# Chunk steps without Q in a hybrid trunk kernel: the inverse goes into b and r_b once, and dense pieces lie in 8 gaps

## What is computed

```python
kk = hd(k * k_k)
kk = kk / jnp.maximum(jnp.linalg.norm(kk, axis=-1, keepdims=True), 1e-12)
k = k * (1 + (a - 1) * k_a)
b_h = kk * a_h
def step(state, inp):          # one token, 16 heads of 64
    r_t, w_t, k_t, v_t, kk_t, b_t = inp
    sa = jnp.einsum('bhvk,bhk->bhv', state, -kk_t)
    state = state * w_t[:, :, None, :] + sa[..., None] * b_t[:, :, None, :] + v_t[..., None] * k_t[:, :, None, :]
    return state, jnp.einsum('bhvk,bhk->bhv', state, r_t)
_, y = lax.scan(step, state0, xs)
y = group_norm(y) * g_lnx + b_lnx
bonus = jnp.sum(r_h * k_h * r_k, -1, keepdims=True) * v_h
return ((y + bonus) * g) @ w_ob
```

## Time and profile before

| | us |
|---|---|
| median of 3 runs | 1109.28 |
| lowest, highest | 1109.05, 1109.8 |
| the profiled execution | 1107.22 |
| its span in the profile | 1105.4 |
| TensorE busy | 1077.7 |
| VectorE busy | 802.7 |
| ScalarE busy | 569.6 |
| GpSimd busy | 72.2 |

### The profile page before, as it was taken

One profiled execution on the slowest core, in us unless ns is written; L12 is line 12 of the kernel. 1 busy time (PEld: TensorE's weight loads), 2 busy tenths in 40 slices (PEclk: granted clock), 3 DMA queues, 4 the chain that ended last, 5 costly groups with the idle time before them and its releaser, 6 DMA issues. The chain is left out here.

```text
span 1105.4 us, 31915 instructions
## 1 busy us (share of the span) xinstructions
PE 1077.7 (97%) x13568; PEld 977.2 (88%) x13568; DVE 802.7 (73%) x1471; ACT 569.6 (52%) x1008; POOL 72.2 (7%) x61
## 2 busy tenths in 40 slices
PE   8999999999999999999999999999999999999996
PEld 8878888888997999998898888888888979999885
DVE  3678787868676877774557887878876778777645
ACT  3653555555544555553246445555565445555531
POOL 0000010101001000000100000202011010000001
PEclk9999999999999999999999999999999999999998
DMA  8533232322564666566474323222326637566661
GB/s 302 166 102 118 72 101 80 95 90 89 191 229 135 211 190 189 186 200 197 134 236 142 121 88 98 89 86 81 98 64 229 210 128 226 189 185 189 210 188 56
DMA packets 45526, 165.58 MB, mean 150 GB/s; under 512 B 5168, under 2 KB 5424, under 8 KB 45136
## 3 DMA queue, kind: packets, MB, share of 16 engines
q1 hardware_dynamic: 42736, 154.03, 43.4%
q0 software_dynamic: 1504, 7.47, 2.2%
q10 hardware_dynamic: 1152, 2.10, 0.6%
HBM read 160.44 MB, written 3.15 MB: 148 GB/s over the span
## 5 line engine op out<-in xcount | busy, mean ns | idle before, releaser
L771 PE MATMUL ps<-x_tok_r,mid_hi 128*128 128x256 f32 x576 | 177.1, 307 | 0.5 <-DVE ring_r L1758 0.5
L773 PE MATMUL ps<-x_tok_r,ring_r 128*128 128x256 f32 x576 | 162.2, 282 | 0.0
L772 PE MATMUL ps<-yb_hi,mid_hi 128*128 128x256 f32 x576 | 162.1, 281 | 0.0
L1758 DVE TENSOR_TENSOR ring_r<-ring,mid_hi 128x1024 fp32r<-128x1024 f32 x80 | 97.2, 1216 | 31.1 <-ACT mid_hi L1342 31.0
L771 PEld LDWEIGHTS ps<-x_tok_r,mid_hi 128*128 128x128 f32 x576 | 108.5, 188 | 9.5 <-issue 1.4
L772 PEld LDWEIGHTS ps<-yb_hi,mid_hi 128*128 128x128 f32 x576 | 108.9, 189 | 0.7 <-issue 0.7
L773 PEld LDWEIGHTS ps<-x_tok_r,ring_r 128*128 128x128 f32 x576 | 108.9, 189 | 0.0
L1342 ACT CAST mid_hi<-ring 128x1024 fp32r<-128x1024 f32 x80 | 83.8, 1048 | 34.3 <-PE ps L773 26.6
L2021 DVE TENSOR_TENSOR rs_ks_r<-ring,tha_kkn_r 128x1024 fp32r<-128x1024 f32 x44 | 53.9, 1224 | 19.9 <-ACT tha_kkn_r L1394 19.7
L2021 DVE TENSOR_TENSOR vs_dC_r<-ring,b_k_r 128x1024 fp32r<-128x1024 f32 x44 | 53.7, 1220 | 17.6 <-ACT b_k_r L1394 17.6
L2021 DVE TENSOR_TENSOR X_Y_r<-ring,arc_r 128x1024 fp32r<-128x1024 f32 x42 | 51.3, 1222 | 19.8 <-ACT arc_r L1394 19.8
(11 more groups left out here) (487 smaller groups left out, 3326.0 us busy)
## 6 DMA issues: line engine op xcount, KB each, us to landing
ring<-stream_dram SPq DMA_DIRECT2D x281, 512.0 KB, 3.7
lora_w<-lora_dram POOLq DMA_DIRECT2D x2, 1536.0 KB, 7.2
W_bt<-rpar_dram POOLq DMA_DIRECT2D x4, 512.0 KB, 5.1
kt_V<-rpar_dram POOLq DMA_DIRECT2D x4, 512.0 KB, 7.1
x_tok<-x_dram SPq DMA_DIRECT2D x2, 512.0 KB, 4.7
v_saved_dram<-vs_dC ACTq DMA_DIRECT2D x4, 256.0 KB, 4.5
x_tok<-x_dram SPq DMA_DIRECT2D x1, 1024.0 KB, 6.2
vf<-v_saved_dram ACTq DMA_DIRECT2D x4, 256.0 KB, 3.8
```

The source lines that it names most:

```text
L771: pe.matmul(dst, lh, rh, start=start, stop=False)
L772: pe.matmul(dst, lh, rl, start=False, stop=False)
L773: return pe.matmul(dst, ll, rh, start=False, stop=stop)
L1758: dve.tensor_tensor(rounded["ring"][:, k, :], ring[:, k, :], f32(mid_hi[m % NM][:, :]), ALU.subtract).then_inc(*dve_mid.inc(l, m))
```

## The change

**No Q.** The last level of the inverse now updates X and leaves Y (the update on VectorE takes the other half of the block). After it one block, `byX`, multiplies X into b for six units (all but the last chunk's) and into r_b for eight, and does the products of r and the keys with V for all eight units. ScalarE copies the results back over `bt` and `rb` (`by_x`, four copies); `rkv_out` is called once, at the second chunk. A chunk step is then Z, and S with y straight from `Zs`. TensorE has 9690 matmuls where it had 9594, ScalarE 966 instructions where it had 982, VectorE 1433 for 1441, GpSimd 93 for 65.

**Gaps.** A round has 23 gaps, 0 to 22: 14 is ahead of `byX`, 15+2c behind Z, 16+2c behind S. The 20 pieces (19 in the last round of a layer) lie in gaps 14 to 21.

**Orders of casts and subtracts.** `mids_up_to` is called twice a chunk on both engines, without the condition on the chunk.

**Norms and bonus.** The norm's power is split on GpSimd into a rounded high part and the rest, both are transposed, and two rounded products of 256 columns spread them (`spread` holds the selecting rows of both). The bonus product is two rounded ones of 512 columns: ScalarE makes the high part (`bonus_high`), GpSimd the low one (`bonus_low`), which needs ScalarE's.

**Decay.** `d_ext` keeps the exponential of the cumulative sum in columns 1 to 64 of each unit with a 1 in column 0, so that the value before a token and the value at it are two views of it; the subtract at L1790 and the exponential at L1421 go.

```diff
-CHUNK_GAPS = ([[14, 14, 14, 15, 17, 17, 18, 18, 19, 19, 20, 20, 21, 21, 22, 22, 23, 23, 24, 24]] * (GROUPS - 1)
-              + [[14, 14, 15, 16, 16, 17, 17, 18, 19, 19, 20, 20, 21, 22, 22, 23, 23, 24, 24]])
+CHUNK_GAPS = ([[14, 14, 14, 15, 15, 16, 16, 17, 17, 18, 18, 18, 19, 19, 19, 20, 20, 20, 21, 21]] * (GROUPS - 1)
+              + [[14, 14, 15, 15, 16, 16, 16, 17, 17, 18, 18, 18, 19, 19, 19, 20, 20, 21, 21]])
...
-GAPS = 14 + 3 * NCH
+GAPS = 15 + 2 * NCH
...
+                whole = rn[:, :].rearrange("p (t j) -> p t j", t=TT)
+                pool.wait_ge(*pool_prep(r, "rn"))
+                pool.tensor_copy(rn_hi, whole).then_inc(*pool_prep.inc(r, "rn_hi"))
+                pool.wait_ge(*pool_prep(r, "rn_hi"))
+                pool.tensor_tensor(rn_lo, whole, f32(rn_hi), ALU.subtract).then_inc(*pool_prep.inc(r, "rn_lo"))
+
+            def bonus_low(r):
+
+                pool.wait_ge(*act_rkk(r, "hi"))
+                pool.tensor_tensor(rkk_lo, flat(tmp), f32(rkk_hi), ALU.subtract).then_inc(*pool_rkk.inc(r, "lo"))
...
+                    bonus_low(r)
+                    if g:
+                        y_rstd(r - 1)
+                        y_out(r - 1)
                     if g + 1 < GROUPS:
...
             def prep_rnT(r):
-                pe.wait_ge(*pool_prep(r, "rn"))
-                pe.transpose(bank(4)[0:8, 128:256], rn[:, :], ident).then_inc(*pe_prep.inc(r, "rnT"))
+                pe.wait_ge(*pool_prep(r, "rn_lo"))
+                for t in range(TT):
+                    mm = pe.transpose(bank(4)[0:8, P + t * P:2 * P + t * P], rn_parts[:, 8 * t:8 * t + 8], ident)
+                mm.then_inc(*pe_prep.inc(r, "rnT"))
 
             def prep_rnx(r):
 
                 pe.wait_ge(*dve_prep(r, "rnT"))
+                pe.wait_ge(exact, 2)
                 for b in range(GB):
-                    for t in range(TT):
-                        j = TT * b + t
-                        mm = pe.matmul(tok(4)[:, b, t * P:t * P + P], C["rowsel"][0:8, j * P:j * P + P], rnT[:, :],
-                                       start=True, stop=True)
+                    mm = pe.matmul(tok(4)[:, b, :], spread[:, b * P:b * P + P], rnT, start=True, stop=True)
                 mm.then_inc(*pe_prep.inc(r, "rnx"))
...
-                pe.wait_ge(*dve_prep(r, "rkk"))
+                pe.wait_ge(*pool_rkk(r, "lo"))
                 pe.wait_ge(*(act_y(r - 1, "yn") if g else dve_att(l, f"lh{g}")))
-                pe.matmul(bank(6), C["bones"], flat(tmp), start=True, stop=True).then_inc(*pe_bonus.inc(r, "bonus"))
+                pe.matmul(bank(6), bones_r, rkk_hi, start=True, stop=False)
+                pe.matmul(bank(6), bones_r, rkk_lo, start=False, stop=True).then_inc(*pe_bonus.inc(r, "bonus"))
...
+                fill(14, 1)
+                pe.wait_ge(*dve_wkv(r, f"X{LEVELS - 1}1"))
                 pe.wait_ge(*act_wkv(r, "ktV"))
+                if g + 1 < GROUPS:
+                    pe.wait_ge(*act_prep(r + 1, "thw"))
+                early = sum([bc(c) for c in range(NCH // 2)], [])
+                late = sum([bc(c) for c in range(NCH // 2, NCH)], [])
+                for i in range(len(early) + NU):
+                    if i < len(step_units):
+                        u = step_units[i]
+                        per_head(unit64(3)[:, u, :], X, bt[:, u, :], u)
+                    elif i < len(step_units) + len(late):
+                        u = late[i - len(step_units)]
+                        per_head(unit64(5)[:, u, :], X, rb[:, u, :], u)
+                    if i < len(early):
+                        u = early[i]
+                        mm = crossed(unit64(2)[:, u, :], X, rb[:, u, :], u)
+                    else:
+                        u = i - len(early)
+                        mm = swapped(rkv64(u % NCH)[:, u // NCH, :], rk[:, u, :], Vc[:, u, :])
+                mm.then_inc(*pe_wkv.inc(r, "byX"))
                 for c in range(NCH):
-                    if c:
-                        pe.wait_ge(*dve_wkv(r, f"S{c - 1}"))
-                    s_old = S[:, (c + 1) % 2, :, :]
                     y = [unit64(5)[:, u, :] for u in bc(c)]
                     if c:
+                        s_old = S[:, (c + 1) % 2, :, :]
+                        pe.wait_ge(*dve_wkv(r, f"S{c - 1}"))
                         for b, u in enumerate(bc(c)):
                             mm = per_head(step64(2)[:, b, :], a_of, s_old[:, b, :], u)
                             if b == GB - 1:
                                 mm.then_inc(*pe_wkv.inc(r, f"Z{c}"))
                             crossed(y[b], r_of, s_old[:, b, :], u, start=(b == 0), stop=False)
-                    fill(14 + 3 * c, c == 0)
-                    pe.wait_ge(*dve_wkv(r, f"Z{c}" if c else f"Y{LEVELS - 1}1"))
-                    if c == 0 and g + 1 < GROUPS:
-                        pe.wait_ge(*act_prep(r + 1, "thw"))
-                    if c == NCH - 1:
-                        pe.wait_ge(*act_wkv(r, "rkV_first"))
-                    for b, u in enumerate(bc(c)):
-                        swapped(rkv64(c)[:, b, :], rk[:, u, :], Vc[:, u, :])
-                        mm = per_head(step64(3)[:, b, :], Y, Zs[:, b, :] if c else akV[:, u, :], u)
-                    mm.then_inc(*pe_wkv.inc(r, f"Q{c}"))
-                    fill(15 + 3 * c)
+                    fill(15 + 2 * c)
                     if g + 1 < GROUPS and c == 0:
                         prep_v(r + 1)
                         prep_rnT(r + 1)
-                    pe.wait_ge(*act_wkv(r, f"Q{c}"))
+                    pe.wait_ge(*(dve_wkv(r, f"Z{c}") if c else act_wkv(r, "rbX")))
                     for b, u in enumerate(bc(c)):
+                        z = Zs[:, b, :] if c else akV[:, u, :]
                         if c < NCH - 1:
-                            mm = per_head(step64(2)[:, b, :], bt, Qs[:, b, :], u)
+                            mm = per_head(step64(2)[:, b, :], bt, z, u)
                             if b == GB - 1:
                                 mm.then_inc(*pe_wkv.inc(r, f"S{c}"))
-                        mm = crossed(y[b], rb, Qs[:, b, :], u, start=(c == 0), stop=(c == 0 or b == GB - 1))
+                        mm = crossed(y[b], rb, z, u, start=(c == 0), stop=(c == 0 or b == GB - 1))
                     mm.then_inc(*pe_wkv.inc(r, f"y{c}"))
                     if g + 1 < GROUPS and c == 0:
                         prep_rnx(r + 1)
-                    fill(16 + 3 * c)
+                    fill(16 + 2 * c)
...
-                act.wait_ge(*dve_prep(r, "cp"))
-                act.activation(flat(dA), flat(dB), ACT.Exp, scale=-DECAY).then_inc(*act_prep.inc(r, "P"))
-                act.activation(flat(dC), flat(dC), ACT.Exp, scale=-DECAY).then_inc(*act_prep.inc(r, "Pp"))
+                act.wait_ge(*dve_prep(r, "cum"))
+                act.activation(d_at, by_unit(dB[:, :, :]), ACT.Exp, scale=-DECAY).then_inc(*act_prep.inc(r, "P"))
                 act.activation(flat(dB), flat(dB), ACT.Exp, scale=DECAY).then_inc(*act_prep.inc(r, "iP"))
...
+            def bonus_high(r):
+
+                act.wait_ge(*dve_prep(r, "rkk"))
+                act.copy(rkk_hi, flat(tmp)).then_inc(*act_rkk.inc(r, "hi"))
...
-            def chunk(r, c):
-                act.wait_ge(*pe_wkv(r, f"Q{c}"))
-                act.copy(Qs[:, :, :], step64(3)).then_inc(*act_wkv.inc(r, f"Q{c}"))
...
+            def by_x(r):
+
+                act.wait_ge(*pe_wkv(r, "byX"))
+                dst, src = [t.rearrange("p (b c) s -> p b c s", b=GB)[:, :, 0:NCH - 1] for t in (bt, unit64(3))]
+                act.copy(dst, src).then_inc(*act_wkv.inc(r, "btX"))
+                dst, crossed, own = [t.rearrange("p (b c) s -> p b c s", b=GB) for t in (rb, unit64(2), unit64(5))]
+                for q, o in zip(HEADS, OTHER):
+                    act.copy(dst[q, :, 0:NCH // 2], crossed[o, :, 0:NCH // 2])
+                act.copy(dst[:, :, NCH // 2:], own[:, :, NCH // 2:]).then_inc(*act_wkv.inc(r, "rbX"))
+
+            def rkv_out(r):
+
+                src = ps[:, 7, :].rearrange("p (c b s) -> p c b s", b=GB, s=CH)
+                dst = yt[:, :, :].rearrange("p (b c) s -> p c b s", b=GB)
+                for q, o in zip(HEADS, OTHER):
+                    last = act.copy(dst[o], src[q])
+                last.then_inc(*act_wkv.inc(r, "rkV"))
...
-                        mids_up_to(l, mids_by(GAPS * g + 13 + 3 * c))
+                        mids_up_to(l, mids_by(GAPS * g + (14 + 2 * c if c else 13)))
                         for kind, i in pairs_done(g, c=c - 1):
                             if kind == "gate":
                                 gate(l, i)
                             elif kind == "rkv":
                                 rkv(l, g + 1, i % 3)
-                        chunk(r, c)
+                        if c == 0:
+                            by_x(r)
+                        mids_up_to(l, mids_by(GAPS * g + 15 + 2 * c))
                         if c == 0 and nxt:
                             prep_exp(r + 1)
```

(45 more changed lines are left out.)

82 lines of the change are left out of this document (44 added, 38 removed).

## The result

The changed kernel took 1115.8 us in the median (1114.9 to 1117.3, 4 runs) against 1109.2 for the kernel before (1107.8 to 1109.8, 4 runs): a ratio of 1.0081, with a 95% interval of 1.0063 to 1.0099. Measured again beside the last experiment, with six runs, it was 1.0095 (1.0077 to 1.0113). It is slower: the medians lie 6.7 and 9.9 us apart, where 1.4 was forecast. The profiled execution of after took 1117.3 (span 1115.5), that of before 1107.2 (span 1105.4).

What follows compares the result with a forecast made beforehand. TensorE's queue was taken to bound the kernel. Stages -1.6, turns +3.3 and +4.95, bonus -3.2, last rounds -1.2 and first preparations -0.9 gave +1.4 on 1109.3: 1110.7 us, range 1102 to 1118.

Steps and rivals of the forecast that it cites:

- own case: Whole kernel: the prediction's main forecast, 1110.7 us, its own range 1107.5 to 1113.5, chance 0.45.
- the unit prices: TensorE timeline costs: run of 12 dense matmuls 1.62 us, 16 small ones 0.39; with nothing late the stage takes 22.15.
- The chunk stage: Gap 14 to end of y3, six rounds with a successor: 23.0 us instead of 23.26, -1.6 in all.
- The two late items: TensorE waits for VectorE's first subtract of weights (+0.37 us) and for S2's adds before Z3 (+0.5).
- The turn: To the next round: a second subtract ahead of y_sum delays gram, +1.1 us x 3 in layer 0, +1.65 x 3 in layer 1.
- The bonus product: Two rounded products take 0.63 us where one fp32 product took 1.02: -0.4 x 8 = -3.2 us.
- Last rounds: Each layer's last round, without next preparation: three runs of dense matmuls fewer, -0.6 x 2 = -1.2 us.
- rival D: S0 waits for ScalarE's four copies by X: +0.5 us x 8 = +4, 1114.7 us; chance 0.10.
- GpSimd's subtract: Bonus low part: added cast and 1.28 us subtract end well before TensorE reaches the bonus; if not, 1.3 us a round.
- rival B: After y_sum, GpSimd's subtract holds VectorE's centring, so the second mask is late: +6.7 us, 1117.4; chance 0.30.
- first preparations: Each layer's first preparation gains from the cheaper spreading of the norms, partly VectorE's: -0.45 x 2 = -0.9 us.
- Rival C: The turn costs nothing because the last cast is done earlier: 1102.4 us, 1097 at the extreme; chance 0.15.

Runs made afterwards that it cites:

- the last experiment: Changed kernel with four edits (y_sum earlier, high part behind centring, a subtract ahead of scaled keys, v's shift behind S2's adds): 1097.2 us, ratio 0.9926.
- the run in fp32: Changed kernel with only the bonus undone: one fp32 product of 512 columns, no high or low part; 1112.3 us, ratio 1.0039 against the kernel before.

## Why the prediction was wrong

The forecast was 1110.7, no change or a little slower; measured were 1115.8 and, in the second measurement, 1116.2. The time lies inside the wide range, 1102 to 1118, but outside the own case's 1107.5 to 1113.5, and the change is five to seven times the +1.4 us of the sum. Point by point:

- **What bounds, and the unit prices: right.** With nothing late the stage takes 22.13 in layer 0 and 22.35 in layer 1, forecast 22.15.
- **The chunk stage: right.** Forecast 23.0, measured 22.87 in layer 0 and 23.12 in layer 1. The two late items are where they were put, at gap 19 (0.47, forecast 0.37) and at Z3 (0.2, forecast 0.5; the first had taken part of the second).
- **The turn: right.** Forecast +1.1 and +1.65, measured from the end of y3 to gram 2.84 for 1.62 (+1.22) and 3.47 for 1.83 (+1.64), together +8.55 for +8.25. The kernel before with this order alone: +7.1 in its turns.
- **The bonus product: right in TensorE's own rows,** -0.41 a round (0.96 to 0.55) for -0.4. Whether the kernel gains all of that is open: the run in fp32 loses only 1 to 2 us of the 3.3.
- **Last rounds: too good by 0.35 each.** Forecast -0.6, measured -0.25. S0 there waits 0.19 us for ScalarE's last copy by X, which ends at 285.30 (the run ahead of it takes 1.81 for 1.62 us), a small form of rival D; the rest is runs of 18 that cost 2.35, not 2.31, and edges.
- **GpSimd's subtract: the step that failed.** The part on the bonus took the new operations on ScalarE and GpSimd as covered, and asked only whether they are ready in time for the bonus product (they "end well before TensorE reaches the bonus"; they did). It set their effect on VectorE apart, as rival B, at 0.30, on the ground that "No row shows VectorE as the one that waits". But the prediction's own figures had GpSimd start at 1.5 and VectorE at 1.62 after `y_sum`, with a row of a stretched GpSimd operation beside a VectorE one. In all six turns it went that way, with a margin of 0.11 us in five and 0.05 in one, for the 0.1 worked out. The centring took 1.71 to 1.77 us for 0.69, and the stretch of TensorE's attention products and small matmuls up to the next dense piece, in which the second mask is waited for, grew from 3.27 to 4.30 us in each of six rounds: +6.2, where the sum had nothing and rival B +6.7. With the high part behind the centring the wait is gone and the kernel 0.6% faster.

By the rows the sum is -1.6 (stages), +8.5 (turns), -3.3 (bonus), -0.5 (last rounds), -0.9 (first preparations, as forecast, not measured apart) and +6.2 (masks): +8.4, beside 7 to 10 measured. That agreement does not confirm each term. Cut at the same places, the second trace of the changed kernel is 8.7 us longer than that of the kernel before: +8.55 in the six turns, +0.05 in the eight stretches from gram to the end of y3 (where late masks stand against shorter stages and bonus products), -0.86 up to the first gram product, +0.64 from layer 0's last y3 to layer 1's first gram product, and +0.3 behind the last y3. So the gain forecast for the first preparations may be there in layer 0 and does not show in layer 1.

The rivals were written as alternatives to the own case, but B is a cost that adds to it, and both it and the turns were there: with it the same working gave 1117.4. A missing row for one direction of a conflict was read as evidence against it. All eight centrings of the kernel before took 0.69 us: nothing of GpSimd's was running when they began.

Rival C did not occur: the cast waits for gap 21's slot as read. D occurs only in the two last rounds; elsewhere ScalarE's last copy ends at 181.25 and S0 starts at 181.34.

What stays open: why the clock fell in round 0 in some executions at a place where no wait of TensorE differs from those in which it did not; why it fell in four of the six long turns and not in the other two; where the +0.64 between the layers comes from; and the size of the bonus term (by the rows 3.3 us, by the run in fp32 1 to 2). That GpSimd's small casts of the norms cost nothing was read from the absence of a wait, not tried apart.

## What to carry to other kernels

Where a change puts work on an idle engine, look for what runs at that moment on the engine that it can hold up (VectorE for GpSimd here), and compare the two start times: 0.1 us decided 6 us here, and an extra small copy in the right place gave them back. In an in-order queue, place an instruction that waits for another engine behind everything the bound engine waits for; here one subtract ahead of `y_sum` cost 7 us in the kernel before and 8.5 in the changed one. When a wait is removed and the next one grows by the same amount, add up the queue between the two points and take work out of it instead of changing its order.

## What the runs showed of the hardware

- VectorE's operation with two SBUF operands (128x512) took 1.71 to 1.77 us instead of 0.69 when a GpSimd operation of two SBUF operands had started 0.05 to 0.11 us before, and GpSimd's took 1.67 instead of 1.28 when VectorE had started 0.17 us before (1.61 at 0.23). The first was not slowed in either case.
- After the waits of TensorE of 2.3 to 2.9 us in the turns of one run (the subtract ahead of y_sum in the kernel before, the cast in its old place), the granted clock fell to 0.5 for about 3 us four times in six. The two waits of 2.0 to 2.1 us that each of the twelve traces has elsewhere (in the kernel before until 359.84 and 908.10) were followed at once by such a fall in 14 of 24 cases, the first in the kernel before among them (0.55 from 360.8 to 364.2). After waits of 1.1 to 1.8 us the clock stayed at 1.00 in all six turns of five kernels. Such a fall costs up to 1.7 us beyond the wait. It also came where no wait over 0.6 us stood in the 10 us before it: in four traces near 119 and once at 734, so a long wait is not the only thing that it follows.
